# Attention scores on the two halves of the array instead of zero-padded keys

## What is computed

```
xn   = rms_norm(h);  proj = xn @ w_in            # q, k, v of both mixers, index q/k, gates
a:   4 heads; p1 = softmax(q1 k1^T), p2 = softmax(q2 k2^T), causal, head size 64
     out = (p1 - lam * p2) @ v                   # differential attention
idx: score[q,k] = sum_h iw[q,h] * relu(iq[q,h] . ik[k])   # 8 index heads, size 64
     top 128 keys of each query -> bias (0 or -1e30)
b:   8 heads, shared k and v of size 64: softmax(q k^T + bias) @ v
h   += (sigmoid(ga) * (a @ w_a) + sigmoid(gb) * (b @ w_b)) @ w_out
h   += PEER(rms_norm(h))                         # product-key experts, most of the time
```

## Time and profile before

| | us |
|---|---|
| median of three executions | 2352.19 |
| lowest, highest | 2349.07, 2356.54 |
| profiled execution, span from first to last instruction | 2344.2 |
| project(), to the first score matmul | 297.3 |
| attend(), scores and values of all heads | 297.3 to 495.5 |

### The profile page before, as it was taken

The page is one execution under the profiler, slowest core; times in us unless marked ns, Lnnn a source line. Parts: engine busy times, 40 slices in busy tenths (PEclk is TensorE's granted clock), DMA queues, the critical chain, the costliest instruction groups (busy, mean ns, idle before and its releaser), DMA issues.

```text
span 2344.2 us, 29842 instructions
## 1 busy us (share of the span) xinstructions
PE 2162.8 (92%) x9791; PEld 1700.9 (73%) x9794; DVE 1218.6 (52%) x3132; ACT 748.8 (32%) x1099; POOL 409.4 (17%) x160
## 2 busy tenths in 40 slices
PE   6799978889899989998998998897999999999998
PEld 5678755554347877777777777776888888888887
DVE  7852569732217289538917963810544444444443
ACT  3322234320013344245234423532322222222221
POOL 3233300000003422432342243232000000000000
PEclk9999969889899999999999999999999999999999
DMA  3122120000203423632662363156655554555542
GB/s 104 69 73 95 49 108 1 37 1 1 98 19 108 148 68 130 224 126 80 205 199 76 121 229 130 67 193 237 218 208 183 194 200 180 205 188 188 205 179 107
DMA packets 164892, 307.63 MB, mean 131 GB/s; under 512 B 9808, under 2 KB 77008, under 8 KB 162016
## 3 DMA queue, kind: packets, MB, share of 16 engines
q1 hardware_dynamic: 164656, 306.81, 37.6%
q10 hardware_dynamic: 176, 0.07, 0.0%
HBM read 237.64 MB, written 69.21 MB: 131 GB/s over the span
## 4 chain that ended last, share of the span: by engine, by line
PE 56%; DVE 5%; DMA 4%; issue 3%; DVEq 2%; POOL 2%; ACT 2%; SPq 1%; POOLq 0%; ACTq 0%
PE psum L1627 30%; PE psum L1299 7%; PE psum L1301 7%; PE psum L1300 7%; DMA u<-in_u 3%; PE psum L1318 3%; PE psum L1265 2%; DVE hot_j L1543 2%; DVE hot_i L1541 2%; POOL ul L1434 2%; ACT uh L1357 1%; DVEq L1541 1%; ACT act_w L1364 1%; DVEq L1543 0%; DMA wq<-in_w_query 0%
## 5 line engine op out<-in xcount | busy, mean ns | idle before, releaser
L1434 POOL TENSOR_TENSOR ul<-u,uh 128x1024 fp32r<-128x1024 f32 x128 | 315.1, 2462 | 1023.5 <-ACT uh L1357 1023.5
L1299 PE MATMUL psum<-xh,uh 128*128 128x512 f32 x1024 | 408.5, 399 | 11.9 <-POOL ul L1434 9.1
L1301 PE MATMUL psum<-xh,ul 128*128 128x512 f32 x1024 | 400.1, 391 | 0.0
L1300 PE MATMUL psum<-xl,uh 128*128 128x512 f32 x1024 | 399.9, 391 | 0.0
L1661 DVE TENSOR_TENSOR vl<-v,vh 128x1024 fp32r<-128x1024 f32 x128 | 156.8, 1225 | 367.1 <-ACT vh L1645 367.1
L1627 PE MATMUL psum<-vh,wh 128*128 128x512 f32 x1024 | 316.0, 390 | 11.3 <-DVE wl L1664 11.3
L1627 PE MATMUL psum<-vl,wh 128*128 128x512 f32 x1024 | 315.7, 389 | 0.0
L1627 PE MATMUL psum<-vh,wl 128*128 128x512 f32 x1024 | 315.7, 389 | 0.0
L1645 ACT CAST vh<-v 128x1024 fp32r<-128x1024 f32 x128 | 135.0, 1055 | 485.1 <-PE psum L1627 472.9
L1541 DVE TENSOR_SCALAR hot_i<-iota,picksT 128x128 f32<-128x128 f32 x512 | 208.8, 408 | 84.0 <-PE psum L1318 47.9
L1299 PEld LDWEIGHTS psum<-xh,uh 128*128 128x128 f32 x1024 | 193.5, 189 | 59.2 <-issue 11.6
(11 more groups left out here) (244 smaller groups left out, 2518.3 us busy)
## 6 DMA issues: line engine op xcount, KB each, us to landing
u<-in_u SPq DMA_DIRECT2D x128, 512.0 KB, 3.6
v<-in_v SPq DMA_DIRECT2D x63, 1024.0 KB, 4.9
act_mat<-act_w SPq DMA_DIRECT2D x128, 256.0 KB, 2.1
gate_mat<-stage SPq DMA_DIRECT2D x32, 1024.0 KB, 4.6
gate<-gate_mat SPq DMA_DIRECT2D x63, 512.0 KB, 5.6
act_v<-act_mat SPq DMA_DIRECT2D x63, 512.0 KB, 6.4
wraw<-in_w_wide SPq DMA_DIRECT2D x18, 1024.0 KB, 5.2
w_out<-in_w_out SPq DMA_DIRECT2D x1, 4096.0 KB, 17.0
```

The lines of the kernel that those rows point to most:

```text
L1299: nc.tensor.matmul(bank(m, 4 + k), uh[:, k, c], m.xh[:, c], start=(c == 0), stop=False)
L1300: nc.tensor.matmul(bank(m, 4 + k), uh[:, k, c], m.xl[:, c], start=False, stop=False)
L1301: last = nc.tensor.matmul(bank(m, 4 + k), ul[:, k, c], m.xh[:, c], start=False, stop=(c == DC - 1))
L1434: nc.gpsimd.tensor_tensor(ul[:, k], u[:, k], uh[:, k].bitcast(F32), ALU.subtract).then_inc(s["u_low"], 1)
```

## The change

- akT, bkT and ikT lose the axis of 2: each key is stored once, on the same 64 partitions as its head's queries (the small keys, shared by the heads, stand on both halves). The zero fills, their semaphore and the wait go, and turn_out copies all 128 partitions at once.
- A score contracts over 64 partitions: rows_half() gives the lower or the upper half (by s for "a", by the head's parity otherwise), and both operands are sliced to it.
- score_of() takes a list of scores. It issues the query-key matmuls of all of them first, and then the mask matmuls with their semaphores. The wait for the bias now stands between the two.
- scores_at() makes the lists: the two scores of an "a" head, for tiles 0 to 2 two "b" heads at the even head (nothing at the odd one), and one "b" head at a time in tile 3. Index scores go in pairs.
- w_a gets its own place, and SP loads it right after w_out without a wait.

```diff
-    m.akT = sb("akT", [P, 2, 4, KEYS])
-    m.bkT = sb("bkT", [P, 2, KEYS])
-    m.ikT = sb("ikT", [P, 2, KEYS])
+    m.akT = sb("akT", [P, 4, KEYS])
+    m.bkT = sb("bkT", [P, KEYS])
+    m.ikT = sb("ikT", [P, KEYS])
...
-            nc.gpsimd.memset(m.akT[:], 0.0)
-            nc.gpsimd.memset(m.bkT[:], 0.0)
-            nc.gpsimd.memset(m.ikT[:], 0.0).then_inc(keys_zeroed, 1)
...
-            act.wait_ge(keys_zeroed, 1)
...
                 if kind == "small":
-                    for k, half in enumerate(halves):
-                        nc.scalar.copy(m.bkT[half, k, key_lo:key_lo + r], ps[half, 0])
-                        last = nc.scalar.copy(m.ikT[half, k, key_lo:key_lo + r], ps[half, 1])
-                    last.then_inc(turned_out, 1)
+                    nc.scalar.copy(m.bkT[:, key_lo:key_lo + r], ps[:, 0])
+                    nc.scalar.copy(m.ikT[:, key_lo:key_lo + r], ps[:, 1]).then_inc(turned_out, 1)
                 elif kind == "ak":
-                    for k, half in enumerate(halves):
-                        last = nc.scalar.copy(m.akT[half, k, :, key_lo:key_lo + r], ps[half])
-                    last.then_inc(turned_out, 1)
+                    nc.scalar.copy(m.akT[:, :, key_lo:key_lo + r], ps).then_inc(turned_out, 1)
...
-    w_a = placer(nc, m.keys_at, m.keys_at + 4 * 2 * 4 * KEYS)("w_a", [P, 4, D])
+    w_a = sb("w_a", [P, 4, D])
...
-            sp.wait_ge(scored, SCORE[(NT - 1, "a", A_HEADS - 1, 1)] + 1)
             sp.dma_start(w_a[:], d.w_branch_a).then_inc(weights, 16)
...
+            def rows_half(key):
+
+                _, kind, h, s = key
+                k = s if kind == "a" else h % 2
+                return slice(k * HEAD, (k + 1) * HEAD)
+
+            def score_of(keys):
+
+                for key in keys:
+                    i, kind, h, _ = key
+                    n = SCORE[key]
+                    w = keys_of(i)
+                    before = SCORE_BANKS[n][1]
+                    if before >= 0:
+                        pe.wait_ge(scores_used, before + 1)
+                    if kind == "idx":
+                        block_, q, k = h // 2, m.iqT, m.ikT
+                    elif kind == "a":
+                        block_, q, k = h, m.aqT, m.akT[:, h]
+                    else:
+                        block_, q, k = h // 2, m.bqT, m.bkT
+                    half = rows_half(key)
+                    ps = score_bank(n)
+                    for c in range(0, w, 512):
+                        e = min(w, c + 512)
+                        last = nc.tensor.matmul(ps[:, c:e], q[half, block_, i * P:(i + 1) * P], k[half, c:e],
+                                                start=True, stop=kind == "idx", skip_group_check=True)
+                    if kind == "idx":
+                        last.then_inc(scored, 1)
+                for key in keys:
+                    i, kind, _, _ = key
+                    if kind == "idx":
+                        continue
+                    w = keys_of(i)
+                    ps = score_bank(SCORE[key])
                     if kind == "b":
+                        pe.wait_ge(bias_ready, i + 1)
...
+            def scores_at(k):
+
+                i, kind, h = ALL_UNITS[k]
+                if kind == "a" or keys_of(i) > 512:
+                    return scores_of_unit(i, kind, h)
+                return [(i, "b", h, 0), (i, "b", h + 1, 0)] if h % 2 == 0 else []
```

More of the change, by code:

```diff
@@ L227, in project @@
     pool_consts = nc.alloc_semaphore("pool_consts")
-    keys_zeroed = nc.alloc_semaphore("keys_zeroed")
     squared = nc.alloc_semaphore("squared")
@@ L492, in turn_out @@
                 key_lo = columns_of(i)
-                halves = [slice(0, HEAD), slice(HEAD, P)]
                 if kind == "small":
-                    for k, half in enumerate(halves):
-                        nc.scalar.copy(m.bkT[half, k, key_lo:key_lo + r], ps[half, 0])
-                        last = nc.scalar.copy(m.ikT[half, k, key_lo:key_lo + r], ps[half, 1])
-                    last.then_inc(turned_out, 1)
+                    nc.scalar.copy(m.bkT[:, key_lo:key_lo + r], ps[:, 0])
+                    nc.scalar.copy(m.ikT[:, key_lo:key_lo + r], ps[:, 1]).then_inc(turned_out, 1)
                 elif kind == "ak":
-                    for k, half in enumerate(halves):
-                        last = nc.scalar.copy(m.akT[half, k, :, key_lo:key_lo + r], ps[half])
-                    last.then_inc(turned_out, 1)
+                    nc.scalar.copy(m.akT[:, :, key_lo:key_lo + r], ps).then_inc(turned_out, 1)
                 else:
@@ L777, in score_of @@
                     if kind == "b":
-                        last = nc.tensor.matmul(ps[:, c:e], m.ident_b[:], bias[:, i % 2, c:e], start=False, stop=True,
-                                                skip_group_check=True)
-                if kind == "a":
+                        pe.wait_ge(bias_ready, i + 1)
                     for c in range(0, w, 512):
-                        f, e = max(c, w - P), min(w, c + 512)
-                        if f < e:
+                        e = min(w, c + 512)
@@ L785, in score_of @@
+                        if kind == "b":
+                            last = nc.tensor.matmul(ps[:, c:e], m.ident_b[:], bias[:, i % 2, c:e], start=False,
+                                                    stop=True, skip_group_check=True)
+                        elif max(c, w - P) < e:
+                            f = max(c, w - P)
                             last = nc.tensor.matmul(ps[:, f:e], m.ident_b[:], m.tri_b[:, f - (w - P):e - (w - P)],
                                                     start=False, stop=True, skip_group_check=True)
-                last.then_inc(scored, 1)
+                    last.then_inc(scored, 1)
@@ L817, in value @@
                 last.then_inc(valued, 1)
-            for h in range(IDX_HEADS):
-                score_of(0, "idx", h, 0)
+            def scores_at(k):
[3 more added lines that the diff above has]
+                return [(i, "b", h, 0), (i, "b", h + 1, 0)] if h % 2 == 0 else []
+            for h in range(0, IDX_HEADS, 2):
+                score_of([(0, "idx", h, 0), (0, "idx", h + 1, 0)])
             for k in range(len(ALL_UNITS) + 3):
                 if k < len(ALL_UNITS):
-                    for key in scores_of_unit(*ALL_UNITS[k]):
-                        score_of(*key)
+                    score_of(scores_at(k))
                 if k >= 3:
@@ L829, in _ @@
                 if k < len(ALL_UNITS):
-                    for key in scores_beside(*ALL_UNITS[k]):
-                        score_of(*key)
+                    score_of(scores_beside(*ALL_UNITS[k]))
             def turn_outs(i):
```

1 line of the change is left out of this document (removed).

## The result

The changed kernel takes 2396.2 us (median of four, 2390.65 to 2399.54) against 2350.6 us for the kernel before (median of four as well, 2347.78 to 2356.54): ratio 1.0176, 95% interval 1.0144 to 1.0208. It is 45 us slower; 2353 us were predicted, with 2343 to 2364 as the range. The profiled execution has a span of 2392.6 us, 48.4 more than before.

A forecast was written before the change was run, and what follows sets the result against it. TensorE's matmuls in later, untouched blocks were over half the chain; attention stretches were bound by VectorE or TensorE. Stretch terms from -0.9 to +1.5 us summed to +0.8, giving 2353 us, range 2343 to 2364.

The forecast's parts named there:

- The likeliest case: Whole kernel: the forecast's own sum, with the clock by stretch as before, 2353 us, no change; chance 0.52.
- the low clock: Rival: half-row scores leave the clock low in tile 1, +11 us, 2364 us, later some 20 more; chance 0.17.
- b1: Sparse heads of the second query tile: score matmuls hidden, -0.5 us, then VectorE is the bound.
- b0: Sparse heads of the first query tile, TensorE-bound at clock 0.50: passes hidden and saved against switches, -0.5 us.
- b3: Sparse heads of the last query tile, TensorE-bound: round 3.56 instead of 3.22 us, +0.8 us in all.
- a1: Second query tile's differential attention with the next tile's index scores: -0.8 us; where the low-clock rival would be decided.
- Part 1: Scores on halves instead of zeros: one pass of overlap a pair, bounds 0 and 2; nothing in tile 3.
- rival of full overlap: Score pairs: halves run fully side by side and switches cost nothing, 2342.6 us; chance 0.11.
- Part 2: Switching between 64-row scores and 128-row work: 0.17 us a switch at either clock, bounds 0 and 0.35.
- Part 3: Order of issue: paired scores become ready together, so VectorE's maxima come later; +1.0 us at the last tile's head.
- Part 4: Bias wait moved behind the score matmuls: hides the first scores' passes where TensorE is the bound, -0.96 us in b0.
- Parts 5 and 6: Projection block's fills and copies, and w_a's earlier load: 0 each; bounds -1.0 to 0 and 0 to 0.5 us.

The follow-up runs named there:

- Kernel 1: The changed order of issue with every score over 128 rows and zero-padded keys, against the kernel before: 2360.6 against 2354.9 us, ratio 1.0017.
- kernel 4: The changed order with 64-row scores in tiles 0 to 2 only, tile 3 and its index scores over 128 rows, against the kernel before: 2360.7 us, ratio 1.0037.
- kernel 2: The kernel before, its order kept, with every score over its own 64 rows: 2439.4 us, ratio 1.0363.
- experiment 6: The kernel before, with only the sparse-head scores of heads 4 to 7 of tile 3 over 64 rows: 2356.1 us, one execution.

## Why the prediction was wrong

**The likeliest case.** I gave the low clock 0.17 and ran the sum at the clock of before. That is the step that failed: every term from b1 on takes a pass or a seam at the level that the stretch had had, while the change itself moves that level. The rows ahead of the prediction had the warning in them. b0 is 98% busy and at 0.50, so a full queue does not by itself bring the clock up; what work it is must matter. Kernel 1, the same order over 128 rows, takes 2360.6 us, within the full range; the 36 us from there to 2396.2 are what the term left at nothing costs.

**The rival's price.** "Half as long again", with b1 +11 and b3 some 20 more, 2364 to 2385 us. Measured: the round of b3 goes from 3.22 to 6.47 us, and to 6.06 us with no seam in it (65 and 80 rows). That is 1.88 times and not 1.5. Of the times that I had taken as fixed, the weight loads of value() in b3 grow from 191 ns on average to 325 (80 rows). I also let it end with b1, where it went on through a2, b2 and a3, and did not count the tail, which alone went from 13.5 us in the earlier trace rows's cut (482.8 to 496.3) to some 20. The point of decision was placed in a1; there the clock did still rise (0.72 against 0.82) and fell again in b1, where kernel 1 has it as low over 128 rows. So the rival named the right cause, but not where it acts: b1 lost 2.9 us and not 11, and not by the rows.

**Part 1, overlap.** One pass saved a pair was the middle of the bounds 0 and 2. It is 2: four records in 1.71 us, in starts of two and two. The Trainium skill, "TensorEngine Tiling (Array Packing)", Theoretical Speedup, gives up to 2x for a dimension of 64 or less, and the timeline agrees. The step that failed is "if matmuls start in order, the second score's pass 1 can run beside the first one's pass 2": the second score's first pass started beside the first one's first pass. "The overlap there is a 16-column pass: nothing", of tile 3, was wrong in the same way for its "a" scores and for the index scores made for it: 2.33 us for a pair where 4.45 would be in turn. My rival of full overlap had that right and still ended on the other side of the result.

**Part 2, seams.** 0.17 us from the 16-row seam. Measured 0.15 at full clock (four seams in 0.59 us) and 0.21 at the low one (0.83 us), where I had taken 0.17 at either: the mechanism right, the size nearly. That a seam might keep the clock low was not so (kernel with seams only).

**Part 3, order.** The delay of the first maximum was priced, the copy that loses its cover was not; it is what makes b0 0.7 us longer instead of 0.5 shorter, and what takes the gain of the pairs in b2 of kernel 4. The order also brings low spells of the clock in b1 (kernel 1), which no term had.

**Part 4, the wait moved.** b0 -0.5 as worked out (19.9 against 20.4). The rest of its 3 us drowns in the spread of the runs.

**Parts 5 and 6.** Right: the first score starts at 297.6 us against 297.3, and w_a's load raises the DMA share of a0 from 0.61 to 0.80 without a wait in the profile. I had it end in b0; the share is 0.00 there, so it ended in a0.

**Open.** When the clock falls is not settled. It fell in b1 over 128 rows too (kernel 1), so pairs over 64 rows are not needed for that; and pairs over 64 rows with short waits between them kept it at 1.00 through b2 of kernel 4. In the changed kernel it rose five more times between 372 and 448 us, with 64-row pairs in the queue, and each time fell again within 7 us; from 447.5 us on it stayed low. So "64-row scores fail to lift the clock" is shown for single scores, in b3 and in kernel 2, and for pairs only that they did not keep it up in a2 and b2 here. Nor is it known why fillers lift b0 over 128-row scores (three a head) and not b3 over 64-row ones (two a head). That rows in use matter is shown for b3 (64, 65 and 80 rows against 96 and 128), with one execution each for 65 and 80, and inferred for a2 and b2 from kernels 1, 2 and 4.

## What to carry to other kernels

Padding with zeros to 128 rows can be the faster form: the zeros cost no time in a matmul of the same columns (round of 3.22 us over 128 rows, 3.23 over 96), and half the rows can cost the clock of everything behind them. Before a change of TensorE's work is summed at the clock of before, name the low spells that the stretch starts from and ask what will end them. When two units are made into a pair, ask what the second one had covered: a wait of 0.5 to 1.3 us for ScalarE's copy took the gain here. Where TensorE waits anyway at the low level and the next stretch is bound by it, matmuls with no purpose in that wait can pay, but only enough of them: one a head did nothing, three made b0 4.1 us shorter than the moved wait alone.

## What the runs showed of the hardware

- Two float32 matmuls on the two halves of the array start together and run side by side, pass by pass: four passes of 400 columns in 1.71 us at the low level instead of 2.88 over 128 rows, and eight records of 512 and 16 columns in 2.33 instead of 4.45.
- A switch between 64 and 128 rows costs 0.15 us at full clock and 0.21 at the low one.
- In the same place of the same kernel, scores over 96 rows were followed by the high level by the third head, scores over 80, 65 and 64 rows stayed at 0.50 through all eight heads and the tail; and 64-row scores begun at the high level stayed there for four heads. In kernel 4 pairs of 64-row scores begun at the high level stayed there through all of b2.
- The low level makes a TensorE-bound round 1.88 times as long (3.22 to 6.06 us).
- Kernels that are the same up to b3 can differ before it: b1 and a2 together took 43.2 us (20.3 + 22.9) in the kernel with 80 rows and 49.9 us (22.9 + 27.0) in the one of experiment 6, with low spells in b1 and a2 in the second only. Most of the spread from 2344 to 2363 us of the kernel before may be that; it was not shown for its own runs.
